# Half as many unread products in three attentions, pooling ahead of the latent attention, and short products grouped

## Chip, cores and metric

The kernel runs on one core of a Trainium2 chip. The metric is the device time of one execution in microseconds (us), the median of several runs. Of the engines, the text calls TensorE PE, VectorE DVE, ScalarE ACT and GpSimd POOL; SP issues the weight transfers.

## What is computed

Two transformer blocks over a sequence of 256 tokens, width 1024, all in 32-bit floats, each with two layers. Only parts of the first block's first layer, and one attention in each layer of the second block, are touched by the change. In the first layer of the first block (64 columns a head, 8 heads, `uc` being the context's projection):

```python
y  = concat([pool_mixer(u[..., :D_POOL], pool_w, pool_scale),
             neighbourhood_attention(q, k, v, k_c, v_c, rpb)]) @ w_out
yc = concat([pool_mixer(uc[..., :D_POOL], pool_w, pool_scale),
             context_attention(qc, k_c, v_c)]) @ w_out
```

`pool_mixer` takes, for four groups of 128 channels, the mean over a window of 2, 4, 8 or 16 tokens, subtracts the token itself, multiplies by a 128x128 matrix and scales. The second block has a causal attention of 8 heads beside a differential one (its first layer), and a sparse attention of 16 heads (its second layer), whose output is a gated sum of three: over compressed tokens (15 keys), over selected tokens and over a window.

## The kernel before

Every engine has its own instruction stream, written as Python that emits it, and the streams wait for each other on semaphores by named events (`pe.wait_ge(*after(event))`). Order on an engine is program order.

**Weights.** SP loads 319 blocks of 1 MB in a fixed order through a ring of four slots (`load_blocks`, L432); a block's load waits until the block four places before it is "used". After the first attentions the order is: two modulation blocks, one block of the output projection `ev_out`, four times over. A modulation block is not multiplied on PE: `mod_chain` (L614, L617) sums its eight slices on DVE, 16 instructions, and PE only adds up the partitions (`mod_sum`, L636), with a lag of four blocks. DVE makes these chains after the context attention, ahead of the first MLP weights.

**An attention** works in units: one head and 128 query tokens. Two heads of one query tile are a pair of units. `att_tensor` (L1000), `att_vector_parts` and `att_scalar` emit the three streams:

- PE: scores of a pair (L1017), two products of 64 rows that use the two halves of the array; transposes of a unit's weights (L1029); products with the values (L1047), 64 output columns for each unit of the pair, each in its own half of the columns.
- DVE: `maxima(u)` reads the scores from PSUM, scales and masks them (L1105, L1107) and takes the negative maximum (L1119, or L1115 in the sparse attention); `weights(u)` takes reciprocals (L1128) and scales (L1142). The order is weights(u), then maxima(u + lead), with lead 2 (4 in the sparse attention).
- ACT: exponentials with their sums (L1175), copies of the transposed weights (L1193) and of the output (L1200). ACT's order within a pair is exponentials of a later even unit, output of the pair before, copy of the even unit, exponentials of the later odd unit, copy of the odd unit.

The score buffers are four (six in the sparse attention), the buffers of transposed weights two. PSUM banks are handed out in turn (`take_bank`), and a bank is written again when its last holder has been read ("taken").

**Unread products.** In an attention with `filled` true, `fill` (L994 to L998) multiplies two constants into a bank that nobody reads. It is 512 columns wide for the first eight calls (`RAISE`) and 256 after that. The latent attention (16 units) has none; the context (16 units), causal (16) and sparse (32) attentions have two for each pair; the differential attention, not paired, has one for each unit. The paired loop on PE is:

```python
for i, pair in enumerate(pairs):
    transposes(pair[0])
    if A.filled:
        fill(2 * i, A.fill_bank)
    transposes(pair[1])
    if i + ahead < len(pairs):
        scores(pairs[i + ahead])
    if A.filled:
        fill(2 * i + 1, A.fill_bank)
    if i == 0 and first_turned is not None:
        first_turned()
    values(pair)
```

**The sparse attention** adds a product of 15 rows (`more_values`, L1046) for the compressed part of each unit into the same sum as the unit's L1047 products.

**Pooling** has 18 DVE steps (`pool_steps`, L1301; `pool_vector`, L1317, L1321, L1323), each waiting for the one before. Twelve are made in the latent attention, one ahead of `weights(u)` for u = 2 to 13, and six in the context attention, u = 2 to 7. PE multiplies the four groups after the context attention (`pool_tensor`, L1331), ACT scales and copies them (`pool_scalar`, L1339), and only then the output projection starts (L933, `project_tensor`), since its first product waits for both "pool_done" and the context attention.

Of the kernel before, what the change touches and what calls it, by code (L numbers as in the profile page):

```python
# [13 lines left out]
P = 128  # L14
# [306 lines left out]
def bass_two_blocks(nc, weights, consts, params, small, bias, pool_inv, x_t, out_t, events):  # L321
    ctx = ExitStack()
    with ctx:
# [40 lines left out]
        def psum(bank, a=0, w=512, rows=slice(0, P)):  # L364
            return ps[rows, bank, a:a + w]
# [628 lines left out]
        def fill(u, b):  # L994


            w = 512 if u < RAISE else 256
            nc.tensor.matmul(psum(b, 0, w), cn("ones"), cn("ident", 0, w), start=True, stop=True)  # L998

        def att_tensor(pe, A, then=None, first_turned=None):  # L1000
# [21 lines left out]
            def transposes(u):  # L1022
                S = att_places(A)[0]
                pe.wait_ge(*after(A.name, "weights", u))
                blocks = A.blocks(u)
                for n in range(0, len(blocks), 4):
                    b = take_bank(pe, (A.name, "turned", u, n // 4))
                    for i, (col, w) in enumerate(blocks[n:n + 4]):
                        ins = nc.tensor.transpose(psum(b, i * P, P, slice(0, w)), S[:, u % A.slots, col:col + w], cn("ident"))  # L1029
                    ins.then_inc(*pe.step(A.name, "turned", u, n // 4))  # L1030

            def values(units):

                T = att_places(A)[1]
                b = take_bank(pe, (A.name, "out", units[-1]))
                for u in units:
                    pe.wait_ge(*after(A.name, "T", u))
                for e in A.values_ready(units[0]):
                    pe.wait_ge(*after(*e))
                blocks = A.blocks(units[0])  # L1040
                for i, (col, w) in enumerate(blocks):
                    for u in units:
                        rows, vs = A.values(u)
                        if i == 0:
                            for value, weight in A.more_values(u):
                                nc.tensor.matmul(psum(b, 0, P, rows), value, weight, start=True, stop=False)  # L1046
                        ins = nc.tensor.matmul(psum(b, 0, P, rows), vs[i], T[0:w, u % 2, i * P:(i + 1) * P],  # L1047
                                               start=(i == 0 and not A.more_values(u)), stop=(i == len(blocks) - 1))
                ins.then_inc(*pe.step(A.name, "out", units[-1]))

            if A.paired:
                pairs = [(u, u + 1) for u in range(0, A.n, 2)]
                ahead = A.lead // 2 + 1
                for i in range(ahead):
                    if i == ahead - 1 and then is not None:
                        then()
                    scores(pairs[i])
                for i, pair in enumerate(pairs):
                    transposes(pair[0])
                    if A.filled:  # L1060
                        fill(2 * i, A.fill_bank)
                    transposes(pair[1])
                    if i + ahead < len(pairs):
                        scores(pairs[i + ahead])
                    if A.filled:
# [4 lines that stand above are left out]
            else:  # L1070
                for i in range(A.n + 3):
                    if i < A.n:
                        scores([i])
                    if 0 <= i - 2 < A.n:
                        transposes(i - 2)
                    if A.filled:
                        fill(i, A.fill_bank)
                    if 0 <= i - 3 < A.n:
                        values([i - 3])
# [80 lines left out]
        def att_vector(v, A, between={}):  # L1160

            opening, rest = att_vector_parts(v, A, between)
            opening()
            rest()
# [136 lines left out]
        def pool_steps():  # L1301


            return [(gi, lv) for gi in range(4) for lv in range(gi + 3)]
# [2267 lines left out]
        def _(eng):  # L3572
# [11 lines left out]
            mod_sum(pe, 0, 7)  # L3584
            pe.at_block = FIRST_MODS
            ev_in_tensor(pe)
            att_tensor(pe, LAT)
            att_tensor(pe, CON)
            pool_tensor(pe)
            cat_ready = lambda k: [("pool_done",), ("context_attention", "done")]  # L3590
            project_tensor(pe, "x01", "ev_out", lambda k: CAT[:, :, k, :], cat_ready, BOTH,
                           banks=range(6),
# [31 lines left out]
        def _(eng):  # L3624
# [4 lines left out]
            EV_IN.high(act, 0)  # L3629
            high_scalar(act, "n1_0", 0, 0, BOTH, BOTH[::-1])  # L3630
            ev_in_scalar(act)
            att_scalar(act, LAT)
            att_scalar(act, CON)
            pool_scalar(act)
            load_table(act, ACT.Sqrt)
            y_out_scalar(act, "x01", BOTH, lambda g: MLP0.high(act, g // 3 - 1) if g in (4, 6) else None)
            root_scalar(act, "y_x01", X, SEQ)
# [53 lines left out]
        def _(eng):  # L3691
# [15 lines left out]
            modulate_vector(v, "n1_0", 0, 0, BOTH, [])  # L3707
            low_vector(v, "n1_0", 0, 0, BOTH, BOTH[::-1])
            ev_in_vector(v)
            pooling = pool_steps()  # L3710
            def pool_next(n):
                for _ in range(n):
                    pool_vector(v, *pooling.pop(0))
            att_vector(v, LAT, {i: lambda: pool_next(1) for i in range(2, 14)})
            att_vector(v, CON, {i: lambda: pool_next(1) for i in range(2, 8)})
            v.stage("norm")
            MLP0.low(v, 0)
            MLP0.low(v, 1)
# [95 lines left out]
```

## Time and profile before

| | us |
|---|---|
| median of 3 runs | 2497.73 (2495.51 to 2498.16) |
| the profiled execution: its own time | 2491.6 |
| its span | 2489.8 |
| PE busy | 2289.7 (92%) |
| DVE busy | 1699.0 (68%) |
| ACT busy | 1008.3 (40%) |
| POOL busy | 43.0 (2%) |
| mean granted TensorE clock | 0.96 of full |

The profile is one execution. A busy engine is one with an instruction in it; PE's ends are modelled. A matrix product of 32-bit floats is shown as two records, so that the 75 unread products appear as 150. A timeline row merges equal instructions that follow each other; its first number is the start and its second the time from the start of the first to the end of the last. In brackets stands how long the engine sat idle before the row, and whom it waited for.

### The profile page before, as it was taken

The page shows a single profiled execution, that of the slowest core. Times are in us where ns is not written, and L with a number is a line of the kernel's source. Part 1 is how long each engine was busy: PE and PEld are TensorE (multiplying, and loading weights), DVE is VectorE, ACT ScalarE, POOL GpSimd, SP SyncE. Part 2 cuts the span into 40 slices and gives each one's busy share as a digit, 9 for nine tenths or more (in the row PEclk, how much of TensorE's full clock was granted, in tenths as well). Part 3 has the DMA queues.
Part 4 walks back from the last instruction along what each step waited for, and adds up shares of the span by engine and source line. Part 5 has one row for each costly group of instructions (what it writes and reads, how often), then busy time and mean ns, then how long its engine had stood idle before and what let it go on. Part 6 is the DMA issues. An engine that isn't in the chain of part 4 may idle for free.

```text
span 2489.8 us, 46467 instructions
## 1 busy us (share of the span) xinstructions
PE 2289.7 (92%) x20192; PEld 1921.8 (77%) x20192; DVE 1699.0 (68%) x3082; ACT 1008.3 (40%) x1763; POOL 43.0 (2%) x53
## 2 busy tenths in 40 slices
PE   7978998999979999999999889898999989998997
PEld 6864487888857678898897889895777779676886
DVE  6968699777647357887763877756356866636586
ACT  2234243322313224544532553434245653534465
POOL 0000000000000000000000000020000011000000
PEclk9999999999989999999999899899889999897999
DMA  8511526656522100000003578550056843003584
GB/s 335 203 52 34 203 103 269 221 220 235 220 93 88 48 1 3 3 3 3 12 4 137 205 271 296 195 186 1 17 203 229 333 182 121 33 1 139 183 324 182
DMA packets 47308, 348.00 MB, mean 140 GB/s; under 512 B 5264, under 2 KB 5280, under 8 KB 5760
## 3 DMA queue, kind: packets, MB, share of 16 engines
q1 hardware_dynamic: 45936, 334.52, 35.8%
q0 software_dynamic: 1168, 10.51, 1.1%
q8 instruction: 159, 2.61, 0.4%
q14 instruction: 45, 0.37, 0.0%
HBM read 343.96 MB, written 1.05 MB: 139 GB/s over the span
## 4 chain that ended last, share of the span: by engine, by line
PE 75%; DVE 16%; ACT 6%; issue 1%; DMA 1%; DVEq 0%; ACTq 0%; SPq 0%; POOLq 0%
PE banks L538 24%; PE banks L2064 6%; PE banks L933 6%; PE banks L2925 3%; PE banks L2926 3%; PE banks L2927 3%; PE banks L787 2%; PE banks L1923 2%; DVE arena L617 2%; PE banks L1737 2%; PE banks L636 2%; PE banks L2141 2%; PE banks L998 1%; PE banks L2956 1%; PE banks L2958 1%; PE banks L2957 1%
## 5 line engine op out<-in xcount | busy, mean ns | idle before, releaser
L617 DVE SCALAR_TENSOR_TENSOR arena<-weight_slots,silu_c,arena 128x256 f32<-128x256 f32 x776 | 314.9, 479 | 0.0
L516 DVE TENSOR_TENSOR moe_w_low<-weight_slots,moe_w_high 128x2048 fp32r<-128x2048 f32 x96 | 218.1, 2289 | 71.6 <-ACT moe_w_high L507 70.7
L507 ACT ACTIVATE mlp_w_high<-weight_slots 128x2048 fp32r<-128x2048 f32 x64 | 122.3, 1910 | 179.4 <-PE banks L538 121.9
L507 ACT ACTIVATE moe_w_high<-weight_slots 128x2048 fp32r<-128x2048 f32 x96 | 181.5, 1911 | 27.2 <-PE banks L2958 19.7
L933 PE MATMUL banks<-arena,weight_slots 128*128 128x256 f32 (+1 forms) x640 | 174.2, 430 | 13.5 <-DVE arena L1797 11.7
L516 DVE TENSOR_TENSOR mlp_w_low<-weight_slots,mlp_w_high 128x2048 fp32r<-128x2048 f32 x64 | 146.3, 2286 | 49.1 <-ACT mlp_w_high L507 49.0
L933 PEld LDWEIGHTS banks<-arena,weight_slots 128*128 128x128 f32 x640 | 123.6, 194 | 58.5 <-issue 44.5
L2064 PE MATMUL banks<-weight_slots,arena 64*64 64x64 f32 (+1 forms) x3648 | 147.1, 223 | 18.9 <-ACT arena L2084 13.3
L2064 PEld LDWEIGHTS banks<-weight_slots,arena 64*64 64x64 f32 x3648 | 139.0, 134 | 27.3 <-ACT arena L2084 15.3
L2925 PE MATMUL banks<-moe_w_high,slots_x 128*128 128x512 f32 x320 | 133.9, 419 | 11.8 <-DVE moe_w_low L516 11.8
L2926 PE MATMUL banks<-moe_w_low,slots_x 128*128 128x512 f32 x320 | 130.1, 406 | 0.0
L2927 PE MATMUL banks<-moe_w_high,slots_x 128*128 128x512 f32 x320 | 129.6, 405 | 0.0
L2292 ACT ACTIVATE weight_slots<-banks 128x512 f32<-128x512 f32 x80 | 46.9, 595 | 120.1 <-DVE weight_slots L2471 94.1
L787 PE MATMUL banks<-arena,constants 128*128 128x256 f32 (+1 forms) x224 | 73.8, 466 | 20.8 <-ACT arena L831 20.8
L2141 PE MATMUL banks<-weight_slots 64*64 64x64 f32 x2560 | 83.6, 220 | 9.3 <-DVE weight_slots L2508 9.3
L2141 PEld LDWEIGHTS banks<-weight_slots 64*64 64x64 f32 x2560 | 78.9, 135 | 11.2 <-DVE weight_slots L2508 11.2
L1175 ACT ACTIVATE arena<-arena 128x256 f32<-128x256 f32 (+2 forms) x128 | 62.3, 488 | 51.3 <-DVE arena L1119 51.1
L2925 PEld LDWEIGHTS banks<-moe_w_high,slots_x 128*128 128x128 f32 x320 | 62.6, 196 | 25.9 <-ACT moe_w_high L507 9.7
L614 DVE TENSOR_SCALAR arena<-weight_slots,silu_c 128x256 f32<-128x256 f32 x184 | 56.2, 348 | 37.7 <-PE banks L636 22.2
L2508 DVE TENSOR_TENSOR weight_slots<-banks,constants 128x512 f32<-128x512 f32 x80 | 54.3, 689 | 40.5 <-PE banks L2064 40.4
L2064 PE MATMUL banks<-arena 64*64 64x64 f32 (+1 forms) x1600 | 77.1, 226 | 0.0
L787 PEld LDWEIGHTS banks<-arena,constants 128*128 128x128 f32 x224 | 47.8, 221 | 37.7 <-issue 26.1
(426 smaller groups left out, 5147.9 us busy)
## 6 DMA issues: line engine op xcount, KB each, us to landing
weight_slots<-weights SPq DMA_DIRECT2D x318, 1024.0 KB, 4.9
arena<-small POOLq DMA_DIRECT2D x1, 2560.0 KB, 9.0
arena<-x_t POOLq DMA_DIRECT2D x1, 2048.0 KB, 9.6
arena<-bias POOLq DMA_DIRECT2D x1, 2048.0 KB, 8.3
constants<-consts POOLq DMA_DIRECT2D x1, 1410.0 KB, 14.3
out_t<-arena SPq DMA_DIRECT2D x1, 1024.0 KB, 3.9
parameters<-params POOLq DMA_DIRECT2D x1, 763.0 KB, 18.1
arena<-pool_inv POOLq DMA_DIRECT2D x1, 512.0 KB, 9.2
```

Source lines behind the costliest of these rows:

```text
L507: nc.scalar.activation(self.pair(j)[0], slot(j, 0, SLOT), ACT.Copy).then_inc(*act.step("high", j))
L516: nc.vector.tensor_tensor(self.pair(j)[1], slot(j, 0, SLOT), self.pair(j)[0], ALU.subtract).then_inc(*v.step("used", j))
L538: ins = nc.tensor.matmul(out, self.pair(j)[part][:, at:at + P], x(k), start=start and n == 0 and k == 0, stop=stop and n == 2 and k == til ...
L617: nc.vector.scalar_tensor_tensor(a_, w, c, a_, ALU.mult, ALU.add).then_inc(*v.step())
L787: ins = nc.tensor.matmul(psum(SUMS_BANK[segs[-1]], 0, len(segs) * SEQ), cn("ones"), squares_of(key, segs, k), start=(k == 0), stop=(k == K ...
L933: ins = nc.tensor.matmul(psum(b, 0, w), slot(j, k, 256, i * P, P), moving(k), start=(k == 0), stop=(k == KT - 1))
L1175: nc.scalar.activation(S[:, u % N, c:c + w], S[:, u % N, c:c + w], ACT.Exp, bias=M[:, u % N, 3 + j:4 + j], accum_out=M[:, u % N, 6 + j:7 + ...
L2064: ins = nc.tensor.matmul(psum(b, n * width, width, r), lhs, rhs, start=(i == 0), stop=(i == len(ts) - 1))
L2141: ins = nc.tensor.matmul(psum(b, p * 64, 64, r), Z[r, p, :], XI[r, p, :], start=False, stop=True, skip_group_check=True)
L2925: nc.tensor.matmul(psum(b), x_hi, wh, start=(k == 0), stop=False)
L2926: nc.tensor.matmul(psum(b), x_hi, wl, start=False, stop=False)
L2927: ins = nc.tensor.matmul(psum(b), x_lo, wh, start=False, stop=(k == KT - 1))
```

## The change

In the paired loop the first of the two unread products is dropped; the second stays, with the widths that `fill(2 * i + 1)` gives. In `values`, the products of `more_values` for both units are issued ahead of the loop over the blocks, and not inside it between the other products; only the sparse attention has any. The 18 pooling steps on DVE come ahead of the latent attention. PE's four pooling products are issued inside the latent attention, at `first_turned` of its first pair: after the transposes of units 0 and 1 and the scores of the third pair, ahead of the first pair's products with the values. ACT's four pooling copies come after its copy of unit 1, ahead of the exponentials of unit 4.

```diff
+                for u in units:
+                    for value, weight in A.more_values(u):
+                        nc.tensor.matmul(psum(b, 0, P, A.values(u)[0]), value, weight, start=True, stop=False)
                 for i, (col, w) in enumerate(blocks):
                     for u in units:
                         rows, vs = A.values(u)
-                        if i == 0:
-                            for value, weight in A.more_values(u):
-                                nc.tensor.matmul(psum(b, 0, P, rows), value, weight, start=True, stop=False)
...
-                    transposes(pair[0])
-                    if A.filled:
-                        fill(2 * i, A.fill_bank)
-                    transposes(pair[1])
+                    for u in pair:
+                        transposes(u)
...
-            att_tensor(pe, LAT)
+            att_tensor(pe, LAT, None, lambda: (pool_tensor(pe), pe.stage(LAT.name)))
             att_tensor(pe, CON)
-            pool_tensor(pe)
...
-            att_scalar(act, LAT)
+            att_scalar(act, LAT, {}, {1: lambda: (pool_scalar(act), act.stage(LAT.name))})
             att_scalar(act, CON)
-            pool_scalar(act)
...
-            pooling = pool_steps()
-            def pool_next(n):
-                for _ in range(n):
-                    pool_vector(v, *pooling.pop(0))
-            att_vector(v, LAT, {i: lambda: pool_next(1) for i in range(2, 14)})
-            att_vector(v, CON, {i: lambda: pool_next(1) for i in range(2, 8)})
+            v.stage("pooling")
+            for gi, lv in pool_steps():
+                pool_vector(v, gi, lv)
+            att_vector(v, LAT)
+            att_vector(v, CON)
```

## Rows read from the trace of the kernel before

**Rows 1.** Windows: PE, PEld, DVE, ACT, POOL busy (count), PEclk, DMA share, GB/s.
```profile
152.70:199.90 47.20, 28.73 (x229) 17.22 (x228) 39.49 (x92) 24.50 (x59) 0.00 (x0) 0.96 0.00 1
200.30:229.80 29.50, 26.92 (x156) 13.88 (x152) 26.39 (x78) 16.09 (x55) 0.00 (x0) 0.94 0.00 1
1721.50:1748.50 27.00, 22.68 (x112) 10.54 (x112) 24.79 (x77) 12.79 (x50) 0.00 (x0) 0.94 0.00 1
2138.00:2210.40 72.40, 70.27 (x502) 45.23 (x502) 48.16 (x172) 41.71 (x157) 0.00 (x0) 1.00 0.00 1
```

**Rows 2.** Waits of DVE in the sparse, then the causal attention: total, times, longest.
```profile
DVE arena L1105 <- PE banks L1017: 9.6, 6, 2.3
DVE arena L1107 <- PE banks L1017: 3.5, 2, 2.8
...
DVE arena L1105 <- PE banks L1017: 0.7, 2, 0.4
```

**Rows 3.** Timeline of DVE, projection to context attention: start, length, instruction, idle before.
```profile
134.04 2.29 DVE L516 TENSOR_TENSOR ev_in_w_low<-weight_slots,ev_in_w_high 128x2048 fp32r<-128x2048 f32 x1
153.94 0.42 DVE L1105 TENSOR_SCALAR arena<-banks 128x256 f32<-128x256 f32 x1 [17.61 <-PE banks L1017]
...
156.72 0.15 DVE L1128 RECIPROCAL arena<-arena 128x1 f32<-128x1 f32 x1
...
158.69 0.15 DVE L1128 RECIPROCAL arena<-arena 128x1 f32<-128x1 f32 x1
...
185.94 0.74 DVE L1317 TENSOR_TENSOR arena<-arena 128x560 f32<-128x560 f32 x1
...
218.44 0.15 DVE L1128 RECIPROCAL arena<-arena 128x1 f32<-128x1 f32 x1
...
219.69 0.15 DVE L1128 RECIPROCAL arena<-arena 128x1 f32<-128x1 f32 x1
...
227.08 0.61 DVE L614 TENSOR_SCALAR arena<-weight_slots,silu_c 128x256 f32<-128x256 f32 x2
...
233.15 0.61 DVE L614 TENSOR_SCALAR arena<-weight_slots,silu_c 128x256 f32<-128x256 f32 x2
```

**Rows 4.** Timeline of PE, latent attention, same columns.
```profile
160.34 2.08 PE L1017 MATMUL banks<-arena 64*128 64x512 f32 x4
...
165.97 1.13 PE L1017 MATMUL banks<-arena 64*128 64x512 f32 x4
```

**Rows 5.** Timeline of PE, context attention and what follows it.
```profile
215.39 0.44 PE L1029 MATMUL banks<-constants,arena 128*128 128x128 f32 x2
...
219.12 0.44 PE L1029 MATMUL banks<-constants,arena 128*128 128x128 f32 x2
...
221.99 0.44 PE L1029 MATMUL banks<-constants,arena 128*128 128x128 f32 x2
...
229.82 3.70 PE L1331 MATMUL banks<-arena 128*128 128x512 f32 x8
234.39 13.97 PE L933 MATMUL banks<-arena,weight_slots 128*128 128x512 f32 x32 [0.87 <-ACT arena L1339]
```

**Rows 6.** Timeline of PE, two pairs in the sparse attention.
```profile
2174.21 0.44 PE L1029 MATMUL banks<-constants,arena 128*128 128x128 f32 x2
...
2181.32 0.43 PE L1046 MATMUL banks<-arena 15*64 15x128 f32 x2
...
2182.40 1.09 PE L1047 MATMUL banks<-arena 128*64 128x128 f32 x14
2183.41 0.44 PE L1029 MATMUL banks<-constants,arena 128*128 128x128 f32 x2
```

**Rows 7.** Windows of two us, latent and context attention (columns of rows 1).
```profile
170.00:172.00 2.00, 1.14 (x8) 0.72 (x8) 1.93 (x6) 0.92 (x4) 0.00 (x0) 1.00 0.00 0
204.00:206.00 2.00, 2.00 (x7) 1.00 (x6) 1.90 (x6) 1.01 (x4) 0.00 (x0) 0.50 0.00 0
```

**Rows 8.** The page's part 6: issues of the weight blocks, KB each, us to landing.
```profile
weight_slots<-weights SPq DMA_DIRECT2D x318, 1024.0 KB, 4.9
```

## The prediction, made before the changed kernel ran

> **What bounds the kernel now.** The page says PE 92% busy, but a share over the span does not tell what each touched stage is worth, so I read four stages by themselves with the windows view [rows 1], then who waits for whom on DVE [rows 2], then the timelines for the period of a pair. Four different limits appear.
>
> The latent attention: DVE 39.5 of 47.2 us, PE 28.7. DVE sets the pace. The context attention, up to 229.8: PE 26.9 of 29.5 and a wait inside it only at the start; PE sets the pace, with DVE close behind. The causal attention: DVE 24.8 of 27.0, and it waits 0.7 us in all for PE's scores [rows 2]. DVE sets the pace, PE's extra products lie beside it. The sparse attention: PE 70.3 of 72.4, and DVE waits 9.6 + 3.5 = 13.1 us for PE's scores. PE sets the pace, and 13.1 us is about the most that a faster PE can give before DVE is the limit.
>
> **Pooling steps off DVE's attention path.** A step takes 0.74 us [rows 3]; two kinds of four are about 0.05 shorter. A unit without a step takes 158.69 - 156.72 = 1.97 us in the latent attention. There 12 steps go, 12 x 0.72 = 8.6 us at most. Their new place is DVE's idle time of 17.6 us between the last weight split (ends 136.3) and the first scores (153.9) [rows 3]. Eighteen dependent steps at 0.74 plus some 0.05 between them are 14.3 us, ending near 150.6: hidden, with 3 us to spare. Were the spare gone, each missing us would delay the first maximum by one.
>
> **Pooling products in the latent attention.** Four products of 512 columns took 3.7 us at full clock [rows 5], and PE gets them after the third pair's scores, near 162.4, where it used to start the values [rows 4]. The clock was at half there (the scores took 2.08 us against 1.13 later [rows 4]), so I take 3.4 + 0.5 = 3.9 us, ending about 166.2. Behind them wait the values of the first pair, the transposes of the second and the scores of the fourth; on ACT the exponentials of unit 4 wait behind four pooling copies, until about 167.0. I walked the three queues through this: weights of unit 4 start near 167.9, the fourth pair's scores arrive near 169.3, and DVE reaches weights of unit 6 at 172.7. Before, with five steps made, it was there at about 172.9. So the first five steps' saving pays for the products, and the other seven remain: 5.1 us. From there a pair has a DVE period of 3.95 us against about 3.2 us of PE work, with scores arriving just in time; I take 0.3 us off for that. **Latent attention: 4.8 us** (bounds: 2, if the products block for 3 us more; 8.6, if nothing blocks).
>
> **Products no longer after the context attention.** PE's pooling starts at 229.82 and the projection at 234.39, 4.57 us [rows 5]. Now the projection waits only for the last output copy, some 0.5 us after 229.82. **4.1 us** (bounds 3.7 to 4.4).
>
> **Context attention, eight unread products fewer.** A pair's period is 3.73 us with two wide products and 2.87 us with two narrow ones [rows 5]. The difference, 0.86, is one wide product's price (two times one wide less one narrow, which is half), so a narrow one costs 0.43. New periods on PE: 2.87 wide, 2.44 narrow; DVE's is 2 x 1.25 = 2.50 [rows 3], now without its six steps. Three full pairs save 0.86 each (2.6), the first, cold one about 0.9, three narrow ones 0.37 (DVE then limits), the last about 0.9 more with the tail, where a product stood between two transposes. **5.5 us** (bounds: 4, DVE and the chain through ACT hold the narrow pairs; 6.8, all eight products' price and the cold one's surplus).
>
> **After it.** The projection starts a run of dense products to about 301 with no PE wait in it, so that run moves by the sum, 4.8 + 4.1 + 5.5 = 14.4 us, to about 220.0. What it needs must move too. DVE's first modulation chain starts at 227.08 [rows 3]; DVE ends only about 4.8 + 4.6 = 9.4 us earlier, at 217.7. The second projection block is loaded once two chains of 6.07 us [rows 3] are done (229.8) and lands 4.9 us later [rows 8], at 234.7. PE wants it after one block's products, 13.97 us [rows 5], and a short sum: 234.5. Just late; I subtract **0.3**. Later chains wait for PE, not PE for them.
>
> **Causal attention.** Eight products fewer on PE, 3.4 + 1.7 = 5.1 us of it, but DVE waits for PE only 0.7 us, and the last product between transposes adds 0.4 in the tail. **1.2 us** (bounds 0 and 1.8).
>
> **Sparse attention.** Here 4 wide and 12 narrow products go: 3.4 + 5.2 = 8.6 us of PE, the first beside a wait and worth nothing. The grouping: from 2181.32 to 2182.40 three groups of two records take 0.36 us each, while the 14 that follow take 1.01 us up to 2183.41, 0.07 a record [rows 6]. Groups that alternate between 15 and 128 rows don't overlap. Together, the four short records should take some 0.42 us and the others, of one shape, 0.59 (8) or 1.05 (16). A pair's values go from 1.66 or 2.09 to 1.0 or 1.47: **0.6 us a pair**. Bounds: 0, if the short ones overlap with nothing and the transition costs as much; 0.65. I take the upper part, as the long run of one shape is the nearest row. Two pairs now take 2183.41 - 2174.21 = 9.20 us; less 0.86 and 1.2 it is 7.1 on PE. DVE's work in the same time is 9.20 less one wait of 1.35, 7.85, and that limits: 1.4 us gained per two pairs, not 2.1. With wide products (two pairs 10.9): 2.9. Sum: first values 0.6, pair 1 1.5, pairs 2 and 3 2.9, pairs 4 to 12 6.3, tail of three pairs 2.0: 13.3. The loop through ACT (copy, exponentials, copy) leaves some pairs without slack: I take **12.5 us** (bounds 5.8, fills alone; 13.6).
>
> On this grouping the Trainium skill (TensorEngine Tiling (Array Packing), Key Properties) says that a change of tiling mode, not of tile, drains the engine. By that rule two of three changes within a pair's values go and the sum is as taken; by the lower bound above it would be 6.7 us smaller. The 0.36 against 0.07 a record agrees with a drain, though no row here separates drain from serial work.
>
> **The sum.** 4.8 + 4.1 + 5.5 - 0.3 + 1.2 + 12.5 = 27.8 us. The profiled execution, 2491.6 (span 2489.8), would become 2463.8. The median of the runs stands 6.1 us above it, at 2497.7, and gives **2470**.
>
> **Rivals.**
> 1. *The clock falls (slower).* The unread products keep PE busy. If fewer let the granted clock drop from 2.4 to 1.2 GHz in the sparse attention, PE's 7.1 us per two pairs become 7.1 x 2.08 / 1.13 = 13.1 [rows 4], 3.9 more than today's 9.2. All eight such stretches: 31 us lost there against 15.3 gained elsewhere, 2513. It decides from about five of eight stretches. Against: in the latent attention, which has no unread product, the clock is 1.00 with PE 1.14 of 2.00 us busy [rows 7]; it was at 0.50 at 204 to 206, just behind the gap between two attentions [rows 7]. The sparse stretch keeps PE 90% busy. 0.03. The Trainium skill speaks against the change here: TensorE: Matmul & The Clock Gate, Part 4, says transposes don't count as busy for the clock, and transposes are what stays. By it the clock would fall in the latent attention already; the rows at 1.00 disagree.
> 2. *The grouping gives nothing.* The sparse attention gains 5.8, the whole 21.1: 2477. For it: the short ones may be serial for another reason. 0.15.
> 3. *The second projection block or the chains hold PE.* The first part then gains DVE's 9.4, not 14.1: 2475. For it: a margin of nothing. Against: only one block is close. 0.12.
> 4. *No change.* Later weight loads take all. Against: SP waits for uses by PE and DVE, which move along. 0.03.
>
> **How the numbers follow.** The forecast has 0.67; rivals 2 and 3 lie inside the range. Measurement tells 0.2%, 5 us. The bounds together give gains of about 14 (2 + 3.7 + 4 - 1 + 0 + 5.8) to 35 (8.6 + 4.4 + 6.8 + 1.8 + 13.6). All at one end is unlikely, but the runs spread by 3 us; 8 in 10 lie in 2461 to 2483. Faster 0.94, same 0.03, slower 0.03.
>
> **What would show it.** DVE's pooling between 137 and 151; latent attention ending near 195 (199.9); L1331 at about 162.4; projection near 220; two sparse pairs in 7.8 us with DVE without waits; three groups of L1046 and L1047 gone, values 1.0 and 1.5 us; the causal attention nearly as long as before. Wrong: granted clock under 1 inside the sparse attention, an idle PE between 234 and 285, or a DVE wait of over 1 us per pair in the latent attention.

## The result, and the profile after

| | before | changed |
|---|---|---|
| median, us | 2497.81 (4 runs, 2495.51 to 2498.16) | 2462.94 (4 runs, 2460.47 to 2471.13) |
| ratio | | 0.9869, 95% interval 0.9848 to 0.9891 |
| profiled execution: its own time | 2491.6 | 2460.64 |
| its span | 2489.8 | 2458.8 |
| PE busy | 2289.7 | 2261.6 |
| DVE busy | 1699.0 | 1699.3 |
| mean granted TensorE clock | 0.96 | 0.96 |

The changed kernel is 34.9 us faster by the medians and 31.0 by the spans. To see where, the span is cut at seven marks on PE: the first scores of the latent attention, the first scores of the context attention, the first product of the projection behind it, and the first scores and the following projection of the causal and of the sparse attention. Four pieces hold the changed code ("lat", "con", "cau", "spa"). The others hold the same instructions in both kernels. The table is summed from the traces; in brackets is how long the granted clock was at 0.5 (1.2 GHz) in a piece.

```
kernel                start   lat           con           to cau   cau           to spa  spa            to end   span
before                152.7   46.81 (3.4)   34.87 (3.4)   1483.3   33.70 (3.4)   350.9   108.26 (13.7)  279.3    2489.8
changed               150.9   44.13 (10.2)  27.15 (3.4)   1480.9   33.99 (10.2)  350.4    93.90 (13.7)  277.4    2458.8
e1_fills_only         150.4   49.49 (14.6)  33.60 (5.9)   1482.5   33.98 (10.2)  350.5   104.95 (19.9)  280.4    2485.7
e2_group_only         149.9   49.19 (11.4)  34.72 (2.2)   1484.4   35.25 (10.2)  349.5    97.74 (13.7)  276.1    2476.9
e3_pool_only          150.4   42.53 (6.8)   29.28 (0.0)   1486.9   33.69 (3.4)   351.0   108.25 (13.7)  279.2    2481.3
e4_no_fills           152.9   43.70 (6.8)   25.37 (3.4)   1482.7   35.72 (27.0)  352.4    94.46 (20.5)  279.2    2466.4
e5_changed_again      150.5   42.57 (6.8)   25.58 (0.0)   1487.1   34.00 (10.2)  350.5    93.90 (13.7)  277.4    2461.6
e6_products_at_tail   150.1   39.44 (3.4)   27.16 (3.4)   1488.4   33.99 (10.2)  350.5    93.90 (13.7)  277.4    2460.9
e7_products_behind    150.4   39.22 (6.8)   29.62 (0.0)   1483.1   33.99 (10.2)  350.5    93.90 (13.7)  277.5    2458.1
e8_causal_both        150.6   44.14 (10.2)  27.16 (3.4)   1480.9   33.70 (3.4)   350.9    93.90 (13.7)  277.5    2458.9
e9_combined           152.9   39.77 (3.4)   25.37 (3.4)   1482.7   33.69 (3.4)   351.0    93.86 (13.7)  277.5    2456.8
e10_changed_third     152.8   42.53 (6.8)   25.57 (0.0)   1487.1   35.33 (16.3)  353.0    93.86 (13.7)  277.5    2467.7
```

In the changed kernel the four touched pieces sum to 199.17 us, against 223.64 before: 24.5 us. The other 6.5 us of the 31.0 are in pieces whose instructions are the same. The later rows show that such pieces move by themselves: "to cau" lies between 1480.9 and 1488.4. So the pieces decide what each part of the change did, not the totals. They move too: "lat" holds the same instructions in the kernel before, in e1 and in e2, and took 46.8, 49.5 and 49.2 us. A piece is best compared between traces with equal time at 1.2 GHz.

After L1046 the changed kernel's lines stand two lower: L1047 is still the products with the values, L1043 those of `more_values`, and 1105, 1107, 1119, 1128, 1142, 1175, 1193, 1200, 1331 and 1339 are now 1103, 1105, 1117, 1126, 1140, 1173, 1191, 1198, 1329 and 1337.

The windows view of the changed kernel, the four attentions (columns of [rows 1]):

```profile
150.90:195.00 44.10, 33.30 (x233) 20.24 (x232) 31.17 (x80) 27.24 (x62) 0.00 (x0) 0.88 0.00 1
195.80:222.00 26.20, 22.12 (x140) 11.38 (x136) 22.15 (x72) 16.12 (x56) 0.00 (x0) 0.93 0.00 1
1707.50:1734.00 26.50, 20.72 (x94) 9.44 (x94) 23.76 (x73) 12.09 (x48) 0.00 (x0) 0.81 0.00 0
2118.00:2182.00 64.00, 58.45 (x491) 37.17 (x490) 51.44 (x182) 44.41 (x163) 0.00 (x0) 0.97 0.01 1
```

In the latent attention DVE fell from 39.5 us to 31.2 and the stage by less than 3, while PE rose from 28.7 to 33.3 with the clock at 0.88. In the causal one the clock fell from 0.94 to 0.81. In the sparse one DVE, 51.4 of 64.0, is now close to PE's 58.5.

DVE's timeline of the changed kernel, from the first pooling step to the latent attention's fourth pair (columns of [rows 3]):

```profile
134.62 0.75 DVE L1315 TENSOR_TENSOR arena<-arena 128x572 f32<-128x572 f32 x1
...
147.53 0.69 DVE L1321 TENSOR_TENSOR arena<-arena 128x512 f32<-128x512 f32 x1
152.13 0.42 DVE L1103 TENSOR_SCALAR arena<-banks 128x256 f32<-128x256 f32 x1 [3.91 <-PE banks L1017]
...
160.84 0.42 DVE L1103 TENSOR_SCALAR arena<-banks 128x256 f32<-128x256 f32 x1 [1.30 <-PE banks L1017]
...
166.52 0.16 DVE L1126 RECIPROCAL arena<-arena 128x1 f32<-128x1 f32 x1 [2.23 <-ACT arena L1173]
...
168.27 0.42 DVE L1103 TENSOR_SCALAR arena<-banks 128x256 f32<-128x256 f32 x1 [1.06 <-PE banks L1017]
...
171.64 0.15 DVE L1126 RECIPROCAL arena<-arena 128x1 f32<-128x1 f32 x1
...
176.48 0.42 DVE L1103 TENSOR_SCALAR arena<-banks 128x256 f32<-128x256 f32 x1 [0.21 <-PE banks L1017]
...
189.03 0.17 DVE L1126 RECIPROCAL arena<-arena 128x1 f32<-128x1 f32 x1 [0.29 <-ACT arena L1173]
```

Pooling takes 13.6 us and DVE still waits 3.9 us afterwards: it is hidden, as [rows 3] promised. Three waits follow at the start of the attention, 2.23 + 1.06 us of them behind the pooling products. The last weights (189.03) come 38.1 us after the stage's start, against 42.3 before (194.96). So DVE's chain is 4.1 us shorter, but the stage only 2.7.

PE's timeline of the changed kernel, latent attention, context attention and projection:

```profile
158.66 2.08 PE L1017 MATMUL banks<-arena 64*128 64x512 f32 x4
160.67 4.39 PE L1329 MATMUL banks<-arena 128*128 128x512 f32 x8
164.99 1.09 PE L1047 MATMUL banks<-arena 128*64 128x128 f32 x16
...
189.62 1.97 PE L1047 MATMUL banks<-arena 128*64 128x128 f32 x16 [2.14 <-ACT arena L1191]
...
200.78 2.07 PE L998 MATMUL banks<-constants 128*128 128x512 f32 x2
...
206.35 0.65 PE L1029 MATMUL banks<-constants,arena 128*128 128x128 f32 x4
...
209.21 0.66 PE L1029 MATMUL banks<-constants,arena 128*128 128x128 f32 x4
...
212.08 0.66 PE L1029 MATMUL banks<-constants,arena 128*128 128x128 f32 x4
...
221.07 0.66 PE L1047 MATMUL banks<-arena 128*64 128x128 f32 x8 [0.19 <-ACT arena L1191]
222.18 13.97 PE L933 MATMUL banks<-arena,weight_slots 128*128 128x512 f32 x32 [0.46 <-ACT arena L1198]
```

At 189.62 the last but one values take 1.97 us where 164.99 shows 1.09: the clock had fallen at the tail of the latent attention (0.50 in the window from 190 to 192), and it was down again for the context attention's first unread product (2.07 us against 1.12). That is where 1.4 us of DVE's gain went. Wide pairs come every 2.87 us, as forecast, and the projection starts 0.46 us of idle time after the values, not behind 3.7 us of pooling products and their copies: 222.18 against 234.39 [rows 5].

PE's timeline of the changed kernel in the sparse attention, two pairs:

```profile
2145.94 0.43 PE L1043 MATMUL banks<-arena 15*64 15x128 f32 x4
2146.30 0.66 PE L1047 MATMUL banks<-arena 128*64 128x128 f32 x8
2146.89 0.66 PE L1029 MATMUL banks<-constants,arena 128*128 128x128 f32 x4
2147.93 0.66 PE L1029 MATMUL banks<-constants,arena 128*128 128x128 f32 x4 [0.39 <-DVE arena L1140]
...
2149.80 0.43 PE L1043 MATMUL banks<-arena 15*64 15x128 f32 x4
2150.16 1.09 PE L1047 MATMUL banks<-arena 128*64 128x128 f32 x16
2151.18 0.93 PE L1029 MATMUL banks<-constants,arena 128*128 128x128 f32 x4
...
2153.74 0.43 PE L1043 MATMUL banks<-arena 15*64 15x128 f32 x4
```

From 2145.94 to 2153.74 are 7.80 us, 9.20 before. PE now waits for DVE's weights (0.39 us). The four short records take 0.36 us (2149.80 to 2150.16), as long as two took in [rows 6], and 16 of the others take 1.02 us where 14 took 1.01.

How the four fit shows in PE's timeline cut down to the first 0.15 us of a short group, in the kernel before and in the changed one:

```profile
2181.32 0.32 PE L1046 MATMUL banks<-arena 15*64 15x128 f32 x1
```

```profile
2149.80 0.32 PE L1043 MATMUL banks<-arena 15*64 15x128 f32 x2
```

Before, one unit's product runs alone, since the other unit's short product stands behind a product of 128 rows. Now both units' products have started: in the trace their records begin within 0.01 us of each other, each in its half of the columns.

DVE's waits for scores in the sparse attention (2124 to 2173), from the waits view of the changed kernel (columns of [rows 2]), are down from 13.1 us to 2.0:

```profile
DVE arena L1105 <- PE banks L1017: 1.3, 1, 1.3
...
DVE arena L1103 <- PE banks L1017: 0.7, 1, 0.7
```

### The profile page after: what moved, and what is told of

Read it like the earlier page. It is cut to its first block, busy times and chain, and to the rows that moved or that the text cites. A ratio compares the mean times of both kernels' runs of the same rounds, so it can differ in the third digit from the quotient of the medians.

```text
span 2458.8 us, 46345 instructions
## 1 busy us (share of the span) xinstructions
PE 2261.6 (92%) x20128; PEld 1905.7 (78%) x20128; DVE 1699.3 (69%) x3082; ACT 1007.9 (41%) x1763; POOL 43.1 (2%) x53
## 4 chain that ended last, share of the span: by engine, by line
PE 75%; DVE 17%; ACT 6%; issue 1%; DMA 1%; DVEq 0%; ACTq 0%; POOLq 0%
PE banks L538 25%; PE banks L2062 7%; PE banks L933 6%; PE banks L2923 3%; PE banks L2925 3%; PE banks L2924 3%; PE banks L1921 2%; PE banks L787 2%; DVE arena L617 2%; PE banks L1735 2%; PE banks L636 2%; PE banks L2139 2%; PE banks L2954 2%; PE banks L2956 2%; PE banks L2955 2%
## 5 line engine op out<-in xcount | busy, mean ns | idle before, releaser
L933 PE MATMUL banks<-arena,weight_slots 128*128 128x256 f32 (+1 forms) x640 | 174.1, 429 | 13.1 <-DVE arena L1795 11.7
L2062 PEld LDWEIGHTS banks<-weight_slots,arena 64*64 64x64 f32 x3648 | 139.0, 134 | 27.3 <-ACT arena L2082 15.3
```

What stands on the lines that cost most here:

```text
L933: ins = nc.tensor.matmul(psum(b, 0, w), slot(j, k, 256, i * P, P), moving(k), start=(k == 0), stop=(k == KT - 1))
L2062: ins = nc.tensor.matmul(psum(b, n * width, width, r), lhs, rhs, start=(i == 0), stop=(i == len(ts) - 1))
```

## The experiments

**One part each.** The first three kernels are the kernel before with one part of the change. In e1 the first unread product of a pair is gone and nothing else.

```diff
-                    transposes(pair[0])
-                    if A.filled:
-                        fill(2 * i, A.fill_bank)
-                    transposes(pair[1])
+                    for u in pair:
+                        transposes(u)
```

> The kernel before with one part of the change alone: one unread product for a pair, not two. Theory (each part is worth what its stage's limit allows): in the sparse attention PE remains the limit, two pairs go from 9.20 us to 9.20 - 0.86 = 8.34; in the context attention, where DVE still carries six pooling steps, pairs with a step on each unit stay at 2 x (1.25 + 0.74) = 3.98 or so and only the later ones gain; the causal attention gains nothing. In all 7 to 10 us faster than before. Rival (ACT's chain copy, exponentials, copy limits as soon as the product is gone): two sparse pairs stay above 8.6, in all 4 to 6 us. Rival (the clock): more stretches at 1.2 GHz in the attentions with fewer unread products, no gain or a loss.

Measured: 2488.11 us against 2492.93, ratio 0.9983 (0.9973 to 0.9993), 4.8 us faster. The sparse attention gained 3.3 us, and two of its pairs took 8.69. PE's timeline of e1 in the sparse attention:

```profile
2175.37 0.40 PE L1046 MATMUL banks<-arena 15*64 15x128 f32 x2 [0.32 <-ACT arena L1191]
...
2184.06 0.40 PE L1046 MATMUL banks<-arena 15*64 15x128 f32 x2 [0.32 <-ACT arena L1191]
```

Every second pair waits for ACT's copy of the transposed weights: the transposes end earlier, and ACT's copy does not follow as fast. So the products alone are worth less than their own 0.86 us in two pairs: the rival had this right. The other rival had a share: the last 6.2 us of e1's sparse attention ran at 1.2 GHz, which the kernel before does not show there. Up to the end of the last pair but one it had gained 5.1 us. The context attention gained only 1.3 us. DVE still had its six pooling steps there (28.0 us busy of 33.1), and its wide pairs were up to 3.95 us apart, as expected; it also had 5.9 us at 1.2 GHz, not 3.4.

e2 has only the grouping.

```diff
+                for u in units:
+                    for value, weight in A.more_values(u):
+                        nc.tensor.matmul(psum(b, 0, P, A.values(u)[0]), value, weight, start=True, stop=False)
...
-                        if i == 0:
-                            for value, weight in A.more_values(u):
-                                nc.tensor.matmul(psum(b, 0, P, rows), value, weight, start=True, stop=False)
```

> The kernel before with the short products of a sparse pair issued together, nothing else. Theory (every change between products of 15 and of 128 rows costs; three become one): 0.70 us less in each pair's products with the values, as in the changed kernel, and, since PE is the limit there, two pairs at 9.20 - 1.40 = 7.80 us, just where DVE's 7.85 lies; in all 10 to 12 us faster. Rival (the short products are cheap only when the queue has slack, the gain comes with the dropped unread products): under 0.4 us a pair, 6 us or less in all.

Measured: 2479.94, ratio 0.9953 (0.9936 to 0.9969), 13.0 us faster, a little over the 10 to 12 expected; the sparse attention 97.74, 10.5 less. PE's timeline of e2:

```profile
2180.34 0.43 PE L1043 MATMUL banks<-arena 15*64 15x128 f32 x4
...
2188.30 0.43 PE L1043 MATMUL banks<-arena 15*64 15x128 f32 x4
```

Two pairs take 7.96 us, 1.24 less than before, with both unread products still there; DVE's own work, 7.8, is near. The grouping is the largest part of the change, and that it gives nothing (rival 2) is refuted. In the sparse attention the two parts nearly add: to the end of the last pair but one, ahead of e1's stretch at 1.2 GHz, they gain 5.1 and 9.8 us alone and 13.3 together.

e3 has only the pooling, all three moves of it.

```diff
-            att_tensor(pe, LAT)
+            att_tensor(pe, LAT, None, lambda: (pool_tensor(pe), pe.stage(LAT.name)))
             att_tensor(pe, CON)
-            pool_tensor(pe)
...
-            att_vector(v, LAT, {i: lambda: pool_next(1) for i in range(2, 14)})
-            att_vector(v, CON, {i: lambda: pool_next(1) for i in range(2, 8)})
+            for gi, lv in pool_steps():
+                pool_vector(v, gi, lv)
```

> The kernel before with the pooling alone moved (DVE's steps ahead of the latent attention, PE's products and ACT's copies inside it). Theory: the latent attention ends 2.5 to 3 us earlier against its own start, the wait ahead of the projection goes (4.0 us), the context attention is PE-bound with two unread products a pair and gains no more than 1.5; in all 7 to 8 us faster. Rival (the pooling's steps also held the context attention back): 10 us or more.

Measured: 2487.09, ratio 0.9981 (0.9971 to 0.9990), 5.8 us faster, under the 7 to 8 expected. By the pieces it gained more, 4.3 in the latent and 5.6 in the context attention, and "to cau" took 3.6 back. The windows view of e3, the same two attentions:

```profile
150.40:193.00 42.60, 31.77 (x235) 18.89 (x234) 31.14 (x80) 27.14 (x62) 0.00 (x0) 0.92 0.00 1
193.00:222.00 29.00, 26.20 (x161) 14.02 (x160) 22.49 (x73) 16.90 (x58) 0.00 (x0) 1.00 0.00 1
```

4.0 of the 5.6 us are the pooling products that left. The other 1.6 lie in the first pair: e3 ran it at full clock and ended its values 6.9 us after the first scores, the kernel before ran it at 1.2 GHz and ended them at 8.5. Behind it the wide pairs come every 3.73 us in both, so beside a slow first pair the six steps cost nothing. Beside a fast one they do: e2 has them and ends its first values at 7.5, but its wide pairs come every 4.0 us and its last values end at 30.2 us, against 28.8 in e3 and 30.4 before. With the unread products dropped as well, the wide pairs come every 2.87 us, against 3.73 (before, e3) and up to 3.95 (e1): in this stage each part hid what the other gave.

**Where is the limit of dropping products?** e4 is the changed kernel with no unread product in the paired attentions.

```diff
-                    if A.filled:
-                        fill(2 * i + 1, A.fill_bank)
```

> The changed kernel without the second unread product of a pair too; no paired attention has any left. Theory (the clock keeps up on the work itself, as in the latent attention): the granted clock stays at 1.00 in the middle of the context and sparse attentions, the context attention becomes DVE-bound at 2.5 us a pair (its wide pairs take 2.87 now), the sparse one stays at 7.8 us for two pairs; 0 to 4 us faster than the changed kernel. Rival (the unread products hold the clock): stretches at 1.2 GHz inside the sparse attention, which lengthen two pairs there to 11 us and more; 5 to 30 us slower than the changed kernel.

Measured: 2467.72, ratio 0.9907 (0.9890 to 0.9924), 25.2 us faster than before, but no faster than the changed kernel. The context attention is as fast as with one product (25.37). In the causal and the sparse attention it is slower, 35.72 and 94.46; in the sparse one the clock was at 1.2 GHz for 6.8 us more, at its end. The windows view of e4, causal attention:

```profile
1712.00:1734.00 22.00, 15.71 (x73) 8.34 (x73) 18.96 (x54) 8.81 (x35) 0.00 (x0) 0.50 0.00 0
```

The clock stayed at 1.2 GHz for the whole window, with PE busy 71% of it. This is rival 1's mechanism, in the causal attention and with one product fewer than the change leaves. It costs 1.7 us against the changed kernel, little for so long a stretch, since DVE (19.0 of 22.0 us busy) sets the pace there.

**The changed kernel again.** e5 and e10 are the changed kernel unaltered, in two other sets of runs, to learn how firm the pieces are.

> The changed kernel itself, for a second trace and beside the variants on one chip. Every theory: instruction for instruction the same, so what differs from its first trace in the stages (latent attention 44.1 us from its first score to the context attention's, of it 10.2 at 1.2 GHz; causal attention 34.0 us, 10.2 at 1.2 GHz) is not the change's doing. If the half-clock stretches come from fewer unread products, they should stand at the same places with the same lengths.

> The changed kernel for the comparison with the combined one on this chip: 2461 to 2466 us. Theory: the causal attention again has 10.2 us at 1.2 GHz and takes 34.0 us, and the sparse one 93.9.

Measured: e5 2463.93, ratio 0.9884 (0.9859 to 0.9910); e10 2465.67, 0.9894 (0.9875 to 0.9913). The latent attention took 42.57 and 42.53 us, the context attention 25.58 and 25.57, both with less time at 1.2 GHz than in the first trace. e10 missed in the causal attention: 16.3 us at 1.2 GHz and 35.33 us, where the five earlier traces with one unread product have 10.2 and 34.0. The touched pieces gained 24.5, 27.6 and 26.3 us in the three traces, the rest 6.5, 0.6 and -4.3.

**What the pooling products cost in their new place.** e6 puts three of the four at the latent attention's seventh pair and the last at its eighth, with ACT's copies after its copies of units 13 and 15. e7 leaves products and copies behind the context attention, as before, with only DVE's steps moved.

```diff
-            att_tensor(pe, LAT, None, lambda: (pool_tensor(pe), pe.stage(LAT.name)))
+            att_tensor(pe, LAT, turned_hooks={6: lambda: (pool_tensor(pe, range(3)), pe.stage(LAT.name)),
+                                              7: lambda: (pool_tensor(pe, [3]), pe.stage(LAT.name))})
...
-            att_scalar(act, LAT, {}, {1: lambda: (pool_scalar(act), act.stage(LAT.name))})
+            att_scalar(act, LAT, {}, {13: lambda: (pool_scalar(act, range(3)), act.stage(LAT.name)),
+                                      15: lambda: (pool_scalar(act, [3]), act.stage(LAT.name))})
```

> The changed kernel with the four pooling products at another place of the latent attention: three after the seventh pair's transposes, where PE idles 2.1 us, and one after the eighth pair's; ACT's copies behind its copies of units 13 and 15. Theory (the products block scores and exponentials at the entry, some 3.4 us of DVE's waits there, 2.2 and 1.1): DVE waits less than 1.5 us between units 2 and 6, and the latent attention takes 41 to 42 us, not 44.1; the whole 2 to 3 us faster than the changed kernel. Rival (the latent attention is held to 4.1 us a pair by the loop over scores and ACT, the entry is absorbed later): under 1 us. Rival (the tail's products only take the place of the idle time and delay the context attention): the latent attention keeps 44 us.

The edit of e7:

```diff
-            att_tensor(pe, LAT, None, lambda: (pool_tensor(pe), pe.stage(LAT.name)))
+            att_tensor(pe, LAT)
             att_tensor(pe, CON)
+            pool_tensor(pe)
```

> The changed kernel with only DVE's pooling steps moved; PE's four products and ACT's copies stay behind the context attention, as before. Theory: the latent attention takes 40 to 41 us (DVE's 12 steps out, 16 units at 1.97 to 2.0, nothing blocks), and the projection starts 4.0 us later against the context attention's start than in the changed kernel (31.2 us, not 27.2): the move of the products is worth 4.0 less about 3.4. Rival (the entry costs nothing, the latent attention is held by its own loop): 43 us or more.

Measured: e6 2462.70, ratio 0.9872 (0.9852 to 0.9893); e7, a single run, 2459.91. The latent attention takes 39.44 and 39.22 us. PE's timeline of e6 at the tail of the latent attention (its lines are numbered as in the kernel before):

```profile
182.94 2.74 PE L1331 MATMUL banks<-arena 128*128 128x512 f32 x6
185.61 1.09 PE L1047 MATMUL banks<-arena 128*64 128x128 f32 x16
...
187.56 1.02 PE L1331 MATMUL banks<-arena 128*128 128x512 f32 x2
188.56 1.09 PE L1047 MATMUL banks<-arena 128*64 128x128 f32 x16
```

The same three pairs' values in e7:

```profile
181.64 1.09 PE L1047 MATMUL banks<-arena 128*64 128x128 f32 x16 [1.07 <-ACT arena L1191]
...
185.60 1.09 PE L1047 MATMUL banks<-arena 128*64 128x128 f32 x16 [1.84 <-ACT arena L1191]
...
188.55 1.09 PE L1047 MATMUL banks<-arena 128*64 128x128 f32 x16 [0.83 <-ACT arena L1191]
```

The products fill gaps in which PE waited for ACT (1.84 and 0.83 us in e7), and the clock holds, the values at 188.56 taking 1.09 us. So DVE's steps are worth 46.8 - 39.2 = 7.6 us in the latent attention, and the products at the first pair take back 42.55 - 39.2 = 3.3, with 6.8 us at 1.2 GHz in all three traces. At the tail they take back less: from the first to the last of these rows are 7.57 us in e6 and 6.91 in e7, both at full clock, so their price is 0.7 us. The whole pieces differ by only 0.2, because e6 had 3.4 us at 1.2 GHz at its start and e7 6.8. e6's 39.4 us is under the 41 to 42 expected, but e6 as a whole is within the interval of the changed kernel: its context attention has 3.4 us at 1.2 GHz and takes 27.16, and "to cau" is the longest of all. e7 against e5 in the context piece is 29.62 - 25.58 = 4.04 us, the price of the products behind it.

**The causal attention with both products.** e8 is the changed kernel with `fill(2 * i)` back between the transposes there.

```diff
+                    transposes(pair[0])
+                    if A.name == "causal_attention":
+                        fill(2 * i, A.fill_bank)
+                    transposes(pair[1])
```

> The changed kernel with both unread products kept in the causal attention alone. Theory (DVE bounds the causal attention, and its half-clock stretch comes from PE's idle gap ahead of it): 33.5 to 35 us from its first score to the projection, as with one product (34.0) and as before (33.7), with some 3 to 10 us at 1.2 GHz. Rival (fewer products let the clock fall): the stretch shrinks to 3.4 us and DVE's waits for scores to the 0.7 us of before.

Measured, a single run: 2460.69; the causal attention 33.70 us with 3.4 at 1.2 GHz, as before. The windows view of e8, and behind it that of the changed kernel in two parts:

```profile
1707.50:1734.00 26.50, 22.74 (x114) 10.50 (x113) 24.01 (x74) 12.56 (x49) 0.00 (x0) 0.94 0.00 0
```

```profile
1709.00:1718.00 9.00, 8.78 (x29) 3.60 (x28) 7.51 (x24) 3.36 (x13) 0.00 (x0) 0.50 0.00 0
1719.00:1733.00 14.00, 10.01 (x62) 4.99 (x60) 13.02 (x42) 6.81 (x29) 0.00 (x0) 1.00 0.00 1
```

This is what the rival expected: with the second product the half-clock stretch is short again and DVE's waits for scores are back at 0.7 us. It is worth 0.3 us, no more.

**The version that these point to.** e9 joins the tail placement of e6, no unread product in the context attention, and both in the causal one.

```diff
         class ContextAttention(LatentAttention):
             name = "context_attention"
-            filled = True
+            filled = False
```

> The changed kernel with three edits that the traces so far point to: the pooling products in the latent attention's tail (39.4 us there, not 42.6 to 44.1), no unread product in the context attention (25.4 us to the projection without any, 25.6 to 27.2 with one), and both kept in the causal attention (33.7, not 34.0). Theory (stages add): 3 to 6 us faster than the changed kernel on the same chip. Rival (the stages that no edit touches differ by 2 to 8 us from one build to the next with the stretches at 1.2 GHz, and bury it): within 2 us of the changed kernel, with the three stages short as said in the trace.

Measured: 2458.63 (4 runs, 2456.03 to 2458.83), ratio 0.9860 (0.9845 to 0.9875); the changed kernel beside it (e10) 2465.67. The intervals of the two ratios only touch, at 0.9875. Latent and context attention together are 65.14 us, the least of all kernels, against 68.1 to 71.3 for the changed kernel. The medians are 7.0 us apart, more than the 3 to 6 expected. The two profiled executions are 10.9 us apart: these two pieces account for 3.0 (e10's 68.10) and the causal attention for 1.6, of which 1.3 is that e10 missed; "to cau", 4.4 us, and "to spa", 2.0, are the rest, and no edit touches them. I take 3.3 to 4.6 us, 3.0 and the 0.3 to 1.6 of the causal attention, as an estimate of the version's own.

## Why the prediction came out as it did

The forecast of 2463.8 for the profiled execution stands against 2460.64, that of 2470 for the median against 2462.94. The direction and the largest part were right. In the three traces of the changed kernel the touched pieces gained 24.5, 27.6 and 26.3 us, up to 3.3 short of the sum of 27.8. The first totals lie lower for reasons outside that sum: the profiled execution's untouched pieces were 6.5 us shorter, and the median stands 2.3 us above the profiled execution, not the 6.1 that the forecast carried over. That a sum of parts with errors of up to 2.1 us each came out so near is in part luck; by the medians of the three sets the gain is 34.9, 29.8 and 27.3 us.

- **Pooling steps.** Hidden, with 3.9 us to spare, as forecast. 7.6 us in the latent attention (e7) against a ceiling of 8.6, and nothing behind the first pair of the context attention, whose pairs are as far apart with the steps (before) as without (e3).
- **Pooling products in the latent attention: 4.8 us forecast, 2.7, 4.2 and 4.3 measured.** Two steps were too small. The walk through the queues had DVE at the weights of unit 6 0.2 us earlier than before; counted from the stage's start it got there 0.5 us later (171.64 less 150.9, against 172.89 less 152.7), since the products took 4.39 us and not 3.9. In e5 and e10 that is all that was missing. In the first trace the tail of the stage also ran at 1.2 GHz, which no step of the prediction had. That the first pair is a costly place for these products was not seen at all: the tail of e6 has them for 0.7 us, not 3.3.
- **Products gone behind the context attention: 4.1 forecast, 4.0 measured** (e7 against e5).
- **Context attention: 5.5 forecast, 3.7 measured at equal clock.** The values end 26.7 us after the first scores, 30.4 before, with 3.4 us at 1.2 GHz in both. The wide periods were right (2.87, three of them worth 2.6). The first, cold pair gained nothing for a forecast of 0.9, the three narrow ones 0.75 for 1.1, the last 0.4 for 0.9. In e5 and e10 the values end at 25.1, 5.3 us earlier than before, but 1.6 of that is the first pair at full clock. Between e2 and e5, which both have a fast first pair, it is 5.1 us, unread products and pooling steps together.
- **The second projection block: 0.3 lost forecast, nothing measured.** PE goes on without a wait. DVE's first two chains end about 12.1 us after 219.29, at 231.4, and with the 4.9 us of [rows 8] the block is, by estimate, there at 236.3, before PE is through its first 32 records and the sums (236.8). Rival 3 did not come true, by half a microsecond of this estimate.
- **Causal attention: 1.2 forecast, -0.3 measured.** The tail's 0.4 us came, but DVE's waits for PE's scores rose from 0.7 to 1.4 us, since 10.2 us ran at 1.2 GHz, not 3.4. The step that failed is that the extra products lie beside DVE and are free to go. With them back, e8 has 3.4 and 33.70 again, as e9 has with 33.69. The link is not strict: e2, with both products, had 6.8 us at the start and 3.4 at the end, and took 35.25.
- **Sparse attention: 12.5 forecast, 14.4 measured.** The middle is right: 1.40 us in two pairs against 1.4. The terms were 0.6 (first values), 1.5 (pair 1), 2.9 (pairs 2 and 3), 6.3 (pairs 4 to 12) and 2.0 (tail); cut at the end of each pair's values, the two traces give 0.7, 1.5, 3.0, 6.7 and 2.4. The tail was undersized by 0.4, and the 0.8 taken off for the loop through ACT was not needed. That loop does hold pairs in e1, where the products go alone; with the grouping a pair has 0.7 us less of work on PE, and DVE is the limit first. The grouping itself gave 0.71 a pair (1.66 to 0.95) for a forecast of 0.6.
- **The clock (rival 1).** In the sparse attention it did not fall: 13.7 us at 1.2 GHz at its start in both kernels, and 1.00 behind that. With fewer products it did in e1 and e4, for 6.2 and 6.8 us, but only in the last pairs. In the causal attention it did, without deciding anything: with two, one and no unread product the stage ran 3.4 us (before, e3, e8, e9), 10.2 (changed, e1, e5 to e7; 16.3 in e10) and 27.0 us (e4) at 1.2 GHz. One trace is out of line, e2 with two products and 10.2. Counted is the whole stage; its first stretch alone, which starts 5.2 to 5.4 us after the first scores in every trace, is 3.4 us with two (6.8 in e2), 10.2 to 10.3 with one and 23.9 with none. The rival had the mechanism and the wrong stage.

On the grouping, four short records now take the 0.36 us that two took, and the 0.71 us of a pair are two groups of 0.36 that are gone. Two things went with them, and no run separates them: two changes between 15 and 128 rows, and the stretches in which one unit's product ran without the other unit's beside it. An estimate from the rows: in a run of one shape the records of both units start in pairs every 0.109 us, so four take 0.22 and a change adds 0.36 - 0.22 = 0.14. Two changes are then 0.3 of the 0.71 us, and the other 0.4 is that products that ran alone now run beside the other unit's. The short products padded to 128 rows, in the old order, would tell. The Trainium skill (TensorEngine Tiling (Array Packing), Key Properties) has the engine drain at a change of tiling mode; the 0.14 us agrees with that and does not prove it.

The latent attention still held 1.00 in e6 and e9 for all but 3.4 us, with transposes, scores and values alone on PE over most of it; in the first trace of the changed kernel, in e1, e2, e4 and e8 it fell in the tail. The Trainium skill (TensorE: Matmul & The Clock Gate, Part 4) would not have transposes count as busy; e6 and e9 show no fall that would need that rule, and no run here separates transposes from the rest.

Left open: why pieces of identical instructions get different stretches at 1.2 GHz ("lat" of e1 and e2 is that of before and took 49.5 and 49.2 us, not 46.8), and with that why "to cau" moves by up to 7.5 us. Its own time at 1.2 GHz moves with it: the traces with 75.1 to 78.5 us of it took 1480.9 to 1484.4, those with 88.7 to 92.2 took 1486.9 to 1488.4. The runs show this, not what starts it.

## What to carry to other kernels

Issue products of the same row count together, so that products for different halves of the columns stand next to each other: each group between two changes took 0.36 us here with two records or with four, and a reorder of two lines was worth more than all unread products dropped (13.0 us against 4.8). Before moving work onto an engine's queue, ask at which place that engine already waits for another; at a stage's start, where every engine hangs on the first pair, four products cost 3.3 us, and in the gaps at its tail 0.7. Filler products are worth keeping where another engine sets the pace, and worth dropping where PE does; count their effect on the granted clock stage by stage.

## What was not expected of the hardware

- Four matmul records of 15 rows take 0.36 us, the same as two, when records of 128 rows stand on both sides: the four are two units' products in different halves of the columns, and they start within 0.01 us of each other.
- Dropping products that nobody reads can lengthen a stage: in the causal attention the stretch at 1.2 GHz went from 3.4 to 10.2 to 27.0 us with two, one and none a pair, and the stage from 33.70 to 33.99 to 35.72. One trace with two (e2) had 10.2 and 35.25.
- The same instructions, in a long stretch that no edit touched, can run up to 7.5 us longer or shorter from one build to the next. A part worth 3 us can't be read from totals, only from its own stage.
